# The two outer weight sums of the fast feed-forward tiles, made by GpSimd instead of VectorE

## The reference, cut to what matters

```python
def swiglu(h, w1, w3, w2):
    return (jax.nn.silu(h @ w1) * (h @ w3)) @ w2

x = x + 0.5 * rms_norm(swiglu(rms_norm(x, g[0]), ffn_w1[l, 0], ffn_w3[l, 0], ffn_w2[l, 0]), g[1])
```

## Time and profile before

| | |
|---|---|
| median of three runs | 1888.58 us |
| the profiled execution | 1887.73 us |
| its span, first to last instruction | 1885.5 us |
| PE busy | 1865.8 us, 99% |
| VectorE busy | 1358.6 us, 72% |
| ScalarE busy | 857.3 us, 45% |
| GpSimd busy | 49.5 us, 3% |
| granted TensorE clock | 1.0 in all 40 slices |

### The profile page before, as it was taken

One profiled execution on the slowest core, in us unless ns is written; L12 is line 12 of the kernel. 1 busy time (PEld: TensorE's weight loads), 2 busy tenths in 40 slices (PEclk: granted clock), 3 DMA queues, 4 the chain that ended last, 5 costly groups with the idle time before them and its releaser, 6 DMA issues.

```text
span 1885.5 us, 31056 instructions
## 1 busy us (share of the span) xinstructions
PE 1865.8 (99%) x12283; PEld 1712.1 (91%) x12283; DVE 1358.6 (72%) x1875; ACT 857.3 (45%) x1239; POOL 49.5 (3%) x55
## 2 busy tenths in 40 slices
PE   8999999999999999999999999999999999999999
PEld 7899988988889899998998999989988898999888
DVE  6899962487656889993288899822878488999623
ACT  6444452355545544462254444522645464444522
POOL 0000000011100000000000000000000000000000
PEclk9999999999999999999999999999999999999999
DMA  5343333222213333333323343332221222433431
GB/s 169 90 112 94 106 112 103 83 83 74 72 56 101 90 90 100 100 107 100 106 68 100 90 111 107 108 103 84 62 62 56 68 80 78 112 109 92 122 100 46
DMA packets 346871, 174.90 MB, mean 93 GB/s; under 512 B 18478, under 2 KB 345244, under 8 KB 346780
## 3 DMA queue, kind: packets, MB, share of 16 engines
q1 hardware_dynamic: 346016, 172.51, 32.7%
q10 hardware_dynamic: 764, 1.11, 0.2%
HBM read 171.50 MB, written 2.10 MB: 92 GB/s over the span
## 4 chain that ended last, share of the span: by engine, by line
PE 91%; DVE 6%; ACT 1%; issue 1%; POOL 0%; DMA 0%; SPq 0%; DVEq 0%; ACTq 0%
PE acc L1753 21%; PE acc L1754 21%; PE acc L1755 21%; PE duo L1753 8%; PE duo L1755 8%; PE duo L1754 8%; DVE sqs L1213 1%; PE duo L1781 1%; DVE xg L1137 1%; DVE y L1160 1%; PE acc L2004 1%; DVE xT L1167 1%; DVE wl L1102 1%; ACT wh L633 0%; PE duo L1788 0%
## 5 line engine op out<-in xcount | busy, mean ns | idle before, releaser
L1753 PE MATMUL acc<-xg,wh 128*128 128x256 f32 (+1 forms) x1552 | 489.0, 315 | 3.9 <-DVE wl L1102 2.7
L1754 PE MATMUL acc<-xg,wh 128*128 128x256 f32 (+1 forms) x1552 | 482.4, 311 | 0.0
L1755 PE MATMUL acc<-xg,wl 128*128 128x256 f32 (+1 forms) x1552 | 482.4, 311 | 0.0
L1102 DVE TENSOR_TENSOR wl<-raw,wh 128x1024 fp32r<-128x1024 f32 (+2 forms) x204 | 234.6, 1164 | 123.9 <-ACT wh L633 121.0
L1753 PEld LDWEIGHTS acc<-xg,wh 128*128 128x128 f32 x1552 | 296.7, 191 | 23.1 <-DVE wl L1102 3.1
L1754 PEld LDWEIGHTS acc<-xg,wh 128*128 128x128 f32 x1552 | 296.9, 191 | 16.5 <-issue 1.4
L1755 PEld LDWEIGHTS acc<-xg,wl 128*128 128x128 f32 x1552 | 296.7, 191 | 15.8
L633 ACT ACTIVATE wh<-raw 128x1024 fp32r<-128x1024 f32 (+2 forms) x204 | 200.0, 1009 | 123.8 <-PE acc L1755 78.4
L1753 PE MATMUL acc<-hT,wh 128*128 128x512 f32 (+1 forms) x704 | 255.6, 363 | 0.0
L1754 PE MATMUL acc<-hT,wh 128*128 128x512 f32 (+1 forms) x704 | 255.4, 363 | 0.0
L1755 PE MATMUL acc<-hT,wl 128*128 128x512 f32 (+1 forms) x704 | 255.4, 363 | 0.0
(11 more groups left out here) (268 smaller groups left out, 3227.9 us busy)
## 6 DMA issues: line engine op xcount, KB each, us to landing
raw<-in_ffn_w_dram SPq DMA_DIRECT2D x240, 512.0 KB, 4.5
raw<-in_ffn_w_dram SPq DMA_DIRECT2D x32, 384.0 KB, 3.4
raw<-in_moba_w_qkv_dram SPq DMA_DIRECT2D x24, 512.0 KB, 3.8
raw<-in_moba_w_o_dram SPq DMA_DIRECT2D x8, 512.0 KB, 3.7
raw<-in_mla_w_o_dram SPq DMA_DIRECT2D x8, 512.0 KB, 3.9
xin<-in_x_dram SPq DMA_DIRECT2D x4, 512.0 KB, 5.5
raw<-in_mla_w_dq_dram SPq DMA_DIRECT2D x4, 512.0 KB, 3.8
raw<-in_mla_w_uq_dram SPq DMA_DIRECT2D x8, 256.0 KB, 3.0
```

Source lines behind the costliest of these rows:

```text
L1102: v.tensor_tensor(wl[:, slot, 0:tiles], raw[:, slot, 0:tiles], f32(wh[:, slot, 0:tiles]), ALU.subtract).then_inc(w_lo, 1)
L1753: t.matmul(dst, w_h, m_h, start=start, stop=False)
L1754: t.matmul(dst, w_h, m_l, start=False, stop=False)
L1755: return t.matmul(dst, w_l, m_h, start=False, stop=stop)
```

## The change

The two outer sums of every fast tile are taken from VectorE's instruction list and put into GpSimd's, in a loop of their own over the 16 tiles of a block. GpSimd waits, as VectorE did, for the tile's two DMAs and for all splits of the tile before, makes the first sum, waits for it, and makes the second. Operands, shapes, semaphores and counts are the same, and nothing else moves: ScalarE's high part of w3's unit and VectorE's inner sums wait for `ssum_ready` as before, which GpSimd now raises for the first two sums of each tile. VectorE's outer sums for the first fast tile go too.

```diff
+            def weight_sums(st):
+
+                u, G0 = U0[st] + (len(KV_U) if st == KV_ST else 0), FAST * FFN_STAGE[st]
+
+                def sums(f, j, counts):
+                    w, n, slot = tile_unit(u, f), G0 + f - FS, 2 * j
+                    for a in range(2):
+                        pool.wait_ge(raw_full[slot + a], counts[a])
+                    pool.wait_ge(w_lo, w)
+                    g.tensor_tensor(ssum[:, UT:UT + KH], raw[:, slot, 0:KH], raw[:, slot + 1, 0:KH], ALU.subtract
+                                    ).then_inc(ssum_ready, 1)
+                    pool.wait_ge(ssum_ready, 4 * n + 1)
+                    g.tensor_tensor(raw[:, slot + 1, 0:KH], raw[:, slot + 1, 0:KH], raw[:, slot + 1, KH:KD], ALU.add
+                                    ).then_inc(ssum_ready, 1)
+
+                with pool.Fori(FS // 2, KF // 2) as it:
+                    for j in range(2):
+                        sums(2 * it + j, j, [landed[tile_unit(u, FS + j) + a] + 16 * (it - FS // 2) for a in range(2)])
+
             rsqrt(RT0[N_PRE0])
+            weight_sums(0)
             post_norm(N_F0)
...
-                def outer_sums(w, g, slot, counts):
-
-                    for a in range(2):
-                        dve.wait_ge(raw_full[slot + a], counts[a])
-                    dve.wait_ge(w_lo, w)
-                    v.tensor_tensor(ssum[:, UT:UT + KH], raw[:, slot, 0:KH], raw[:, slot + 1, 0:KH], ALU.subtract
-                                    ).then_inc(ssum_ready, 1)
-                    dve.wait_ge(ssum_ready, 4 * g + 1)
-                    v.tensor_tensor(raw[:, slot + 1, 0:KH], raw[:, slot + 1, 0:KH], raw[:, slot + 1, KH:KD], ALU.add
-                                    ).then_inc(ssum_ready, 1)
...
                 w = tile_unit(u, FS)
-                outer_sums(w, G0, 0, counts_of(FS))
                 plain(4)
...
-                def fast(f, j, dst, counts):
+                def fast(f, j, dst):
                     w, g, banks, slot = tile_unit(u, f), G0 + f - FS, tile_banks(j), 2 * (1 - j)
-                    outer_sums(w + 4, g + 1, slot, counts)
                     tile_lo(w + 4, 0, slot)
```

More of the change, by code:

```diff
@@ L603, in _ @@
             rsqrt(RT0[N_PRE2])
+            weight_sums(2)
             post_norm(N_F1)
@@ L607, in _ @@
             rsqrt(RT0[N_CKV])
+            weight_sums(4)
             post_norm(N_F2)
@@ L616, in _ @@
             rsqrt(RT0[N_PRE5])
+            weight_sums(6)
             post_norm(N_F3)
@@ L1321, in tile_lo @@
                     v.tensor_tensor(dst, src, f32(high), ALU.subtract).then_inc(w_lo, 1 + (i == 2))
-                def counts_of(f):
-                    return [landed[tile_unit(u, f) + a] for a in range(2)]
                 w = tile_unit(u, FS)
-                outer_sums(w, G0, 0, counts_of(FS))
                 plain(4)
@@ L1381, in ffn @@
                     for j in range(2):
-                        fast(2 * it + j, j, hid[:, bass.ds(2 * it + j, 1)].rearrange("p a s -> p (a s)"),
-                             [c + 16 * (it - FS // 2) for c in counts_of(FS + j + 1)])
-                fast(KF - 2, 0, hid[:, KF - 2], counts_of(KF - 1))
+                        fast(2 * it + j, j, hid[:, bass.ds(2 * it + j, 1)].rearrange("p a s -> p (a s)"))
+                fast(KF - 2, 0, hid[:, KF - 2])
                 def hidden_lo(i):
```

## The result

| | before | after |
|---|---|---|
| median of five runs each | 1888.58 us | 1897.64 us |
| lowest and highest | 1887.44, 1888.69 | 1896.95, 1898.71 |
| span of the profiled execution | 1885.5 us | 1895.1 us |

The ratio is 1.005, with a 95% interval of 1.0038 to 1.0063: 9 us slower. The forecast was 1895 us, its own range 1891 to 1902.

A forecast was written before the change was run, and what follows sets the result against it. PE was taken to bound the fast tiles at 10.08 us; the change makes VectorE's chain 10.13. The profiled 1887.73 us + 6.6 = 1894.3, so about 1895 us median; own range 1891 to 1902, wider range 1889 to 1918.

The forecast's parts named there:

- The removal is worth nothing: Fast tiles: taking two sums, 1.33 us a tile, off VectorE gains nothing, as PE has no idle time there.
- The two prices: SBUF exclusion: a waiting GpSimd sum ends 1.14 us after VectorE; a waiting 1024-column VectorE split ends 1.07 us after GpSimd.
- Who comes next: After `gated`, GpSimd's first sum gets in before the split of index 0, rather than waiting for both; chance 0.56.
- The period: Fast-tile loop: 3.99 us to the inner sums plus 6.14 us of VectorE work gives 10.13 us, against PE's 10.08.
- From period to time: Fourteen periods make a block's last split of index 2 1.7 us late; PE loses 1.6 to 1.7 us a block.
- the term of 6.6 us: Loss of all four blocks, taken as equal: 4 x 1.65 us, added to the profiled 1887.73 us.
- VectorE's room: Fast tiles: VectorE is busy 9.58 us of each 10.08, leaving only half a microsecond of room.
- What would show it: Trace signs: first sum 1.7 us, second 2.1, split 2.3, VectorE idle 0.8, w2 weight loads waiting over 1 us a block.
- The first fast tile: GpSimd may make its sums behind the x sums' split, 2.6 us, some 3 us before they are needed; no cost.
- kept out: Rival: GpSimd waits until VectorE's run ends; period 10.50 us, 7.2 us late a block, 1917 us; chance 0.24.
- no effect: Rival: sums run freely beside VectorE; chain 8.99 us, PE stays the bound, 1888.6 us; chance 0.12.
- more than serial: Rival: GpSimd loop overheads or sums in `raw` slower than 1.29 us; at period 10.8 us, 1934 us; chance 0.08.

The follow-up runs named there:

- the useless addition: Kernel before, all sums on VectorE, plus one unneeded GpSimd addition of 128x512 per fast tile, released where the changed kernel's sums are: 1919.37 us, ratio 1.0166.
- the loop with the fill: Kernel before plus, per fast tile on GpSimd, a 4-column addition and a 508-column fill that reads nothing: 1887.42 us, ratio 0.9997.

## Why the prediction was right

- **The removal is worth nothing.** Right. With one sum moved VectorE makes one instruction less and PE stays the bound: 1887.85 us against 1887.97.
- **The two prices.** Right to a few hundredths: a waiting sum ends 1.15 and 1.16 us behind VectorE (forecast 1.14), a waiting split of 1024 columns 1.08 us behind GpSimd (1.07).
- **Who comes next.** GpSimd gets in between two VectorE instructions that stand end to end, in all 60 periods inside the loops: 56 first sums take 1.67 to 1.69 us (2.8 us was the mark of the rival), and the four that meet a split of the normed x instead of `gated` (line 1345, formerly 1337) take 2.21. The choice was made with 0.56 against 0.24, on the small powers, and they were the right row. The text counted them wrongly: five take 0.87 us, and with the one at 1012.34 there are six, not seven.
- **The period.** 10.165 us against 10.13. The 0.035 us are in the handovers (the inner sums start 4.02 us behind the split of index 2 instead of 3.99; the 6.14 us behind them are as forecast) and, times 14, make 0.5 us of a block.
- **From period to time.** The last split was forecast 1.7 us late and is 2.20; the loss of a block 1.65 and is 2.2. So the term of 6.6 us is too small by 2.2 us against the 8.8 that the blocks lose, 2.0 of it the 0.035 us of period and the rest rounding. It is still right as a mechanism: lateness behind the loop is paid whole, and the experiment with one addition there shows it apart.
- **VectorE's room.** The prediction read half a microsecond from the busy share; the list of 9.45 us leaves 0.63. The forecast didn't use it, since its 6.14 us were taken from a stretch without waits.
- **What would show it.** As forecast: first sum 1.7 us (1.68 measured), second 2.1 (2.16), split 2.3 (2.32), idle 0.8 (0.85), weight loads waiting for line 1395, formerly 1389, by over 1 us a block (2.15). PE's wait for line 1333 doesn't appear in the list of waits, as forecast.
- **The first fast tile.** Its sums were put behind the splits of the x sums at no cost. In the first block they start at 67.27, among the four splits, and hold them up by 2.2 us (6.82 us for the four against 4.62). Slack swallowed it: the first fast tile's split of index 2 is 0.25 us late, as the first inverse square root of the kernel already is (36.00 against 35.74).

The rivals: *kept out* would have shown 2.8 us for the first sum and 1.29 for the second; *no effect* is refuted by the useless addition; *more than serial* has nothing for it: unblocked, the sum in `raw` takes 1.30 us like the other, and the loop with the fill costs nothing.

The Trainium skill's rule ("SBUF — State Buffer", section "Who interferes with whom"), that two SBUF inputs on VectorE exclude a GpSimd instruction that reads SBUF but not one that only writes, agrees with the traces here: 1.79 us against 0.68 for the useless addition, 0.68 and 0.69 beside the fill. Its sentence that issue order decides agrees too, read for each instruction: GpSimd's sum, whose row starts at 100.39, went before the split, whose row starts at 100.83.

## What to carry to other kernels

In these runs work moved from VectorE to GpSimd wasn't taken off VectorE's chain where GpSimd read SBUF beside VectorE instructions with both inputs there. In such a place add GpSimd's time to the chain as if one engine did it. Move it only beside VectorE instructions with an input in PSUM, or when the chain has room for the whole of it. Room is to be read as the sum of start-to-start distances of an unblocked stretch, not as the period less the idle times shown. And where the work behind a stage has no slack, lateness that the stage itself hides is paid right behind it.

## What the runs showed of the hardware that was not expected

GpSimd gets its turn between two VectorE instructions that stand end to end, and the next one waits for the rest of GpSimd's instruction: 2.32 us instead of 1.22. The prediction held this only for the likelier case; here it was so in all 60 periods. A fill of 508 columns on GpSimd took 0.52 us and did not hold up the VectorE sum over it (0.68 us). GpSimd's wait for itself, with both sums unblocked, costs 0.08 us (171.90 + 1.30 to 173.28), half the 0.15 us between the fill and the causal mask.
